# A Transformer Kernel's Last Down Projection in 1024-Column Superchunks, With a Third of Its k-Tile Pairs as Seven Block Products

## What is computed

```python
hn = _rms(x, norm_ffn[l])
x = x + ((jax.nn.silu(hn @ w_ffn_gate[l]) * (hn @ w_ffn_up[l])) @ w_ffn_down[l]).astype(x.dtype)
```

## Time and profile before

| | |
|---|---|
| median of 3 runs | 2681.32 us (2678.99 to 2684.05) |
| the profiled execution, first to last instruction | 2681.4 us |
| PE busy | 2611.9 us (97%), 12607 matmuls |
| DVE busy | 1574.9 us (59%) |
| ACT busy | 1212.8 us (45%) |
| DMA read | 562.39 MB, 211 GB/s over the span |
| chain that ended last | PE 88%, DVE 5%, DMA 5%, ACT 1% |

### The profile page before, as it was taken

How to read it: one execution, slowest core, us unless ns; L and a number is a source line. 1 busy time by engine, 2 the same in 40 slices (tenths; PEclk the granted TensorE clock), 3 DMA queues, 4 the chain that set the end, 5 groups by cost and what they waited for, 6 DMA issues and landing times.

```text
span 2681.4 us, 31852 instructions
## 1 busy us (share of the span) xinstructions
PE 2611.9 (97%) x12607; PEld 2149.9 (80%) x12607; DVE 1574.9 (59%) x1780; ACT 1212.8 (45%) x1634; POOL 10.8 (0%) x62
## 2 busy tenths in 40 slices
PE   5799999999999999999999999999999999999999
PEld 1478877888888888888888888888888888888887
DVE  0489768877545555555555775555555554455554
ACT  1245554544434444444445654544444444344443
POOL 0000000000000000000000000000000000000000
PEclk7799999999999999999999999999999999999999
DMA  9899639787555556555554674445556555565554
GB/s 390 334 345 330 202 141 366 268 284 273 187 190 188 188 188 204 188 188 189 183 178 151 205 245 141 126 164 182 185 181 199 181 195 189 196 193 190 188 188 141
DMA packets 264754, 566.14 MB, mean 211 GB/s; under 512 B 14271, under 2 KB 37564, under 8 KB 252092
## 3 DMA queue, kind: packets, MB, share of 16 engines
q1 hardware_dynamic: 262100, 562.88, 62.0%
q10 hardware_dynamic: 2538, 1.65, 0.2%
HBM read 562.39 MB, written 2.10 MB: 211 GB/s over the span
## 4 chain that ended last, share of the span: by engine, by line
PE 88%; DVE 5%; DMA 5%; ACT 1%; issue 1%; ACTq 0%; DVEq 0%
PE acc L492 66%; PE acc L3061 4%; PE acc L3064 2%; PE sc L3061 2%; DMA w_raw<-in_w_ada_dram 2%; PE tp L3061 2%; PE tp L531 2%; DVE w_lo L443 2%; DVE acc_ada L1663 2%; PE sc L3064 1%; PE tp L3064 1%; DMA w_raw<-in_w_in_dram 1%; PE acc L2729 1%; DMA w_raw<-in_w_out_dram 1%; PE sc L3233 1%
## 5 line engine op out<-in xcount | busy, mean ns | idle before, releaser
L443 DVE TENSOR_TENSOR w_lo<-w_raw,w_hi 128x1024 fp32r<-128x1024 f32 (+2 forms) x878 | 1053.3, 1217 | 581.4 <-ACT w_hi L438 573.8
L438 ACT ACTIVATE w_hi<-w_raw 128x1024 fp32r<-128x1024 f32 (+2 forms) x878 | 912.9, 1054 | 935.0 <-PE acc L492 657.4
L492 PE MATMUL acc<-w_hi,h_both 128*128 128x512 f32 (+2 forms) x3512 | 971.1, 392 | 13.0 <-DVE w_lo L443 8.5
L492 PEld LDWEIGHTS acc<-w_hi,h_both 128*128 128x128 f32 x3512 | 649.5, 188 | 146.5 <-DVE w_lo L443 9.5
L492 PE MATMUL acc<-w_lo,h_both 128*128 128x512 f32 (+2 forms) x1756 | 539.5, 388 | 0.0
L492 PEld LDWEIGHTS acc<-w_lo,h_both 128*128 128x128 f32 x1756 | 329.9, 188 | 68.1
L492 PE MATMUL acc<-w_hi,f_hi 128*128 128x512 f32 x864 | 268.5, 392 | 0.0
L492 PE MATMUL acc<-w_lo,f_hi 128*128 128x512 f32 x864 | 266.1, 389 | 0.0
L492 PE MATMUL acc<-w_hi,f_lo 128*128 128x512 f32 x864 | 266.0, 389 | 0.0
L492 PEld LDWEIGHTS acc<-w_hi,f_hi 128*128 128x128 f32 x864 | 161.6, 188 | 34.7 <-issue 1.2
L492 PEld LDWEIGHTS acc<-w_lo,f_hi 128*128 128x128 f32 x864 | 162.2, 188 | 33.9
(11 more groups left out here) (463 smaller groups left out, 2002.2 us busy)
## 6 DMA issues: line engine op xcount, KB each, us to landing
w_raw<-in_w_ff_dram SPq DMA_DIRECT2D x128, 1024.0 KB, 5.4
w_raw<-in_w_in_dram SPq DMA_DIRECT2D x108, 1024.0 KB, 5.1
w_raw<-in_w_ada_dram SPq DMA_DIRECT2D x96, 1024.0 KB, 7.4
w_raw<-in_w_ffn_gate_dram SPq DMA_DIRECT2D x44, 1024.0 KB, 5.1
w_raw<-in_w_ffn_up_dram SPq DMA_DIRECT2D x44, 1024.0 KB, 5.1
w_raw<-in_w_ffn_down_dram SPq DMA_DIRECT2D x44, 1024.0 KB, 5.0
w_raw<-in_w_out_dram SPq DMA_DIRECT2D x32, 1024.0 KB, 5.5
w_raw<-in_w_up_fox_dram SPq DMA_DIRECT2D x8, 1024.0 KB, 5.0
```

What stands on the lines that cost most here:

```text
L438: nc.scalar.activation(dst, src, ACT.Copy).then_inc(hi_done, 1)
L443: nc.vector.tensor_tensor(dst, src, hi.bitcast(F32), ALU.subtract).then_inc(lo_done, 1)
L492: last = nc.tensor.matmul(acc[b][:, t, 0:width], st[:, kt, t * P:(t + 1) * P], w[:, slot, kt - 2 * j, 0:width], start=(kt == 0 and n == 0) ...
```

## The change

The four column chunks of a group become two superchunks (`s`) of 1024 columns, each over all k-tile pairs of the group. A load is now two k-tiles x 1024 columns (still 1 MB). A superchunk's four outputs (2 token tiles x 2 column blocks) and four further products fill all eight banks.

Most pairs stay as they were, "eights": eight block products (2 token tiles x 2 k-tiles x 2 column blocks) of three matmuls, two halves of 12. They go to four banks, `sc[1]`, `acc[g][0]`, `acc[g][1]`, `sc[0]`, where g is the pair of the moment and u the other. Of the 12 (10) pairs of a group, 4 (3) are "sevens": seven products, of sums of activation blocks and sums of weight blocks (Winograd's form of Strassen's product), in four halves of 6, 6, 6 and 3 matmuls. They use the same four banks for three of them and `acc[u][0]`, `acc[u][1]`, `tp[0]`, `tp[1]` for the other four. The order of pairs is two eights and a seven in turn, then what is left, a seven last; in the last superchunk of all, the last two pairs are exchanged, so that an eight is last.

What comes with it:

- for each seven VectorE makes four 512-element sums of the weight blocks and seven block remainders in place of four; ScalarE makes seven block copies in place of four;
- for each chunk j that feeds a seven, ScalarE and VectorE make the activation sums during the gate and up products of chunk j + 1 (two 512-element copies, four 128-element sums, one 512-element remainder);
- at the end of a superchunk ScalarE copies all eight banks to `down_m` (3 copies behind the split of the next superchunk's or gate chunk's first half, 5 behind that of its second, `down_copies`), and VectorE adds them to `x` in seven instructions behind the splits of halves 2 to 6 (`down_adds`): two of 512 and five of 1024 elements;
- TensorE starts the first half of the next superchunk, or of the next group's first gate chunk, when both `acc[g]` banks are copied;
- the last superchunk is added by `down_last`, and the output leaves in three stores, the last two of 512 KB after the last matmul.

The diff, cut to its core (the tile placements, the sync engine's source patterns and renamed semaphores are left out):

```diff
+        def seven_pairs(size):
+            return list(range(1, 2 * (size - 2), 2))
+
+        def down_order(size, last):
+            seven = seven_pairs(size)
+            eight = [p for p in range(2 * size) if p not in seven]
+            order = []
+            for p in seven:
+                take = 2 if p != seven[-1] else len(eight)
+                order += [(q, False) for q in eight[:take]] + [(p, True)]
+                eight = eight[take:]
+            if last:
+                order[-2:] = order[:-3:-1]
...
-                weights(A["w_ffn_down_2"][0], 4, 4 * size, row0=f0 * CW, uniform=0)
+                for s in range(2):
+                    order, halves = down_order(size, f0 > 0 and s == 1)
...
+            def down_copies(idx, last, a, part):
...
+                if part == 0:
+                    act.wait_ge(S("down_added"), 7 * idx)
+                todo = (((0, 5, sc[1], copied), (1, 0, u_[:, 0, :], u_free), (1, 2, g_[:, 0, :], g_free)),
+                        ((2, 6, u_[:, 1, :], u_free), (2, 3, g_[:, 1, :], g_free), (3, 1, tp[0], copied),
+                         (3, 7, tp[1], copied), (4, 4, sc[0], copied)))[part]
+                for halves_gone, to, bank, free in todo:
+                    act.wait_ge(half_used, last + halves_gone)
+                    nc.scalar.activation(down_m[:, to, :], bank, ACT.Copy).then_inc(free, 1)
...
+                        if last and at == len(order) - 2:
+                            u = (n.acc + 1) % 2
+                            for nth, to in ((0, 0), (1, 6)):
+                                act.wait_ge(half_used, n.half + h0 + nth + 1)
+                                nc.scalar.activation(down_m[:, to, :], acc[u][:, nth, :], ACT.Copy).then_inc(acc_free[u], 1)
...
+            def down_adds(idx, s, a, k):
+                if k == 2:
...
+                    V.tensor_tensor(down_m[:, 1, :], down_m[:, 0, :], down_m[:, 1, :], ALU.add).then_inc(added, 1)
+                    dve.wait_ge(g_free, 2 * (a // 2) + 2)
+                    V.tensor_tensor(x_halves(0, s), x_halves(0, s), down_m[:, 2:4, :], ALU.add).then_inc(added, 1)
+                elif k == 3:
...
+                    V.tensor_tensor(down_m[:, 7, :], down_m[:, 1, :], down_m[:, 7, :], ALU.add).then_inc(added, 1)
+                    V.tensor_tensor(x_halves(1, s), x_halves(1, s), down_m[:, 4:6, :], ALU.add).then_inc(added, 1)
+                elif k == 4:
...
+                    V.tensor_tensor(x_halves(0, s), x_halves(0, s), down_m[:, 0:2, :], ALU.add).then_inc(added, 1)
...
+            def down_last(half, a, h_seven, h_eight):
...
+                dve.wait_ge(half_used, half + h_seven + 3)
+                dve.wait_ge(u_free, used + 1)
+                link(V.tensor_tensor(down_m[:, 1, :], down_m[:, 0, :], tp[0], ALU.add))
+                link(V.tensor_tensor(down_m[:, 7, :], down_m[:, 1, :], tp[1], ALU.add))
+                V.tensor_tensor(x_halves(0, 1), x_halves(0, 1), down_m[:, 0:2, :], ALU.add)
+                link(V.tensor_tensor(x_halves(1, 1), x_halves(1, 1), twice_wide(down_m[:, 7, :]), ALU.add))
+                dve.wait_ge(u_free, used + 2)
+                xr = x[:, :, 3 * CW:D]
+                link(V.tensor_tensor(xr, xr, twice_wide(down_m[:, 6, :]), ALU.add))
+                dve.wait_ge(half_used, half + h_eight + 2)
+                V.tensor_tensor(x_halves(0, 1), x_halves(0, 1), g_[:], ALU.add).then_inc(S("down_added"), 1)
+                V.tensor_tensor(x_halves(1, 1), x_halves(1, 1), sc_both[:], ALU.add).then_inc(S("down_added"), 1)
...
+                        V.tensor_tensor(sums_w[:, 1, :], block[:, 3, :], block[:, 1, :], ALU.subtract).then_inc(summed, 1)
+                        V.tensor_tensor(block[:, 1, :], block[:, 1, :], block[:, 0, :], ALU.subtract).then_inc(summed, 1)
+                        lo_half(0, block[:, 0:4:2, :])
+                        after(h0)
+                        dve.wait_ge(summed, 4 * sevens + 2)
+                        V.tensor_tensor(sums_w[:, 0, :], block[:, 3, :], block[:, 1, :], ALU.subtract).then_inc(summed, 1)
+                        lo_half(1, block[:, 1:4:2, :])
+                        after(h0 + 1)
+                        dve.wait_ge(summed, 4 * sevens + 3)
+                        V.tensor_tensor(block[:, 2, :], block[:, 2, :], sums_w[:, 0, :], ALU.subtract).then_inc(summed, 1)
+                        lo_half(2, sums_w[:])
+                        after(h0 + 2)
+                        lo_half(3, block[:, 2:3, :], 1)
+                        after(h0 + 3)
...
+                        if at == 0:
+                            pe.wait_ge(acc_free[n.acc % 2], 2 * (n.acc // 2))
...
+                        pe.wait_ge(lo_done, h.val(1))
+                        three(m1, both, 2 * pair, slice(0, P), h.slot(RING), 0, opens, ends)
+                        three(m2, both, 2 * pair + 1, slice(0, P), h.slot(RING), 1, False, closes).then_inc(half_used, 1)
+                        pe.wait_ge(lo_done, h.val(2))
+                        three(m5, form[0], nth, all_of, (h + 1).slot(RING), 0, opens, ends)
+                        three(m3, form[3], nth, all_of, (h + 1).slot(RING), 1, False, closes).then_inc(half_used, 1)
+                        pe.wait_ge(lo_done, h.val(3))
+                        if opens and s == 0:
+                            wait_hidden(use + 2 * (done + size))
+                        three(m6, form[1], nth, all_of, (h + 2).slot(RING), 0, opens, ends)
+                        three(m7, form[2], nth, all_of, (h + 2).slot(RING), 1, opens, ends).then_inc(half_used, 1)
+                        pe.wait_ge(lo_done, h.val(4))
+                        three(m4, both, 2 * pair + 1, slice(P, T), (h + 3).slot(RING), 0, False, closes).then_inc(half_used, 1)
```

More of the change, by code:

```diff
@@ L308, in build @@
         hid_banks = ((acc[1], sc_both), (acc[0], tp_both))
+        def seven_pairs(size):
[10 more added lines that the diff above has]
+                order[-2:] = order[:-3:-1]
+            out, half = [], 0
+            for p, is_seven in order:
+                out.append((p, is_seven, half))
+                half += 4 if is_seven else 2
+            return out, half
         row = {}
@@ L1563, in after_gate @@
                                 act_norm_first(jj)
+                            elif jj < 2:
+                                down_copies(1, n.half - 4, n.acc - 2, jj)
                         elif jj == 5:
-                            hidden_out(j + -1)
+                            hidden_out(j + -1, forms)
+                        elif jj == 7 and forms:
+                            act.wait_ge(S("forms_made"), j.times(4).val(4 * seven_before - 1))
+                            nc.scalar.activation(sf_hi[:, bass.ds((j + -1).val(), 1), :, :], f_sums[:].unsqueeze(1),
+                                                 ACT.Copy).then_inc(S("forms_copied"), 1)
                     def after_up(jj):
@@ L1594, in _, with after @@
                 n.acc += 2 * size
-                weights(4, 4 * size, lambda c: None, uniform=0,
-                        first=lambda j: hidden_out(At(size - 1)) if j == 5 else None)
+                for s in range(2):
+                    last = g == 1 and s == 1
+                    order, halves = down_order(size, last)
+                    def after(k):
+                        if s == 0:
+                            if k == 5:
+                                hidden_out(At(size - 1))
+                        elif k < 2:
+                            down_copies(2 * g, n.half - 4, n.acc - 2, k)
+                    for at, (pair, is_seven, h0) in enumerate(order):
+                        h, L = At(n.half + h0), At(n.load + at)
+                        block = raw[:, L.slot(RING)]
+                        if not is_seven:
+                            for j in range(2):
+                                split_hi(act, h + j, L, j, w_hi[:, (h + j).slot(RING)], block[:, 2 * j:2 * j + 2, :])
+                                after(h0 + j)
+                            continue
+                        split_hi(act, h, L, 0, w_hi[:, h.slot(RING)], block[:, 0:4:2, :])
+                        after(h0)
+                        act.wait_ge(S("w_summed"), 4 * sevens + 2)
+                        split_hi(act, h + 1, L, 1, w_hi[:, (h + 1).slot(RING)], block[:, 1:4:2, :])
+                        after(h0 + 1)
+                        act.wait_ge(S("w_summed"), 4 * sevens + 3)
+                        split_hi(act, h + 2, L, 1, w_hi[:, (h + 2).slot(RING)], sums_w[:])
+                        after(h0 + 2)
+                        act.wait_ge(S("w_summed"), 4 * sevens + 4)
+                        split_hi(act, h + 3, L, 1, w_hi[:, (h + 3).slot(RING), 0:1], block[:, 2:3, :])
+                        after(h0 + 3)
+                        sevens += 1
+                        if last and at == len(order) - 2:
[3 more added lines that the diff above has]
```

(8 more changed lines are left out.)

199 lines of the change are left out of this document (169 added, 30 removed).

## The result

| | before | after |
|---|---|---|
| median | 2681.43 us (2678.20 to 2684.82, 9 runs) | 2687.4 us (2684.95 to 2691.81, 9 runs) |
| profiled execution, span | 2681.4 us | 2683.0 us |
| last transposes of group 0 to the last add | 2225.30 us to its end: 452.92 us | 2220.43 us to its end: 459.39 us |
| TensorE in that stretch / last add behind the last matmul | 451.59 / 1.33 us | 456.72 / 2.67 us |

The ratio is 1.0021, interval [1.0011, 1.0030]: **slower by 6.0 us**. The forecast was slower by 14.0, to 2695.3; the time is in the range's lowest part.

What follows compares the result with a forecast made beforehand. The prediction took TensorE's unbroken matmuls, 0.2267 us each, to bound the kernel. It summed -9.5 + 6.6 + 11.4 + 2.2 + 1.3 + 2.0 = +14.0 us, to 2695.3 us on the median, range 2687 to 2702.

Steps and rivals of the forecast that it cites:

- the last eight: Last pair: TensorE waits 1.3 us because ScalarE copies two banks ahead of splitting it.
- the end: After the last matmul: VectorE's last adds end 3.1 to 3.2 us behind it instead of 1.26, costing 2.0 us.
- -9.5: Saving in the sevens: 42 matmuls fewer at 0.2267 us each, 9.5 us less.
- the two figures: Skill page's 512-column matmul times, 131 ns sustained and about 216 ns alone; by them the saving would be 5.5 or 9.1 us.
- The start of a superchunk: Second superchunks and group 1's first gate chunk: TensorE waits for ScalarE's bank copies, 3 x 2.2 us.
- The first seven of a second superchunk: Each group's second superchunk: delayed halves and the previous superchunk's adds make TensorE wait for VectorE, 2 x 5.7 us.
- first seven of a first superchunk: Each group's first superchunk: the seven's third half, made behind hidden_out, comes late, 2 x 1.1 us.
- The bounds: Whole change: +17.4 us with slower copies and 512-element work, +4.6 us if VectorE's SBUF work ran at one-operand pace.
- rival B: Half the cost is covered, by one-operand pace or free adds: 2684 to 2686 us, about no change; chance 9%.
- A: Ring covers nearly all, TensorE hardly waiting at sevens and starts: 2673.8 us, faster; chance 5%.
- C: Clock falls too, 1.6 us each at three starts and behind two slow sevens: 2700 to 2703 us; chance 6%.
- the 3.42 us at 100 us: Stretch without a matmul in the trace before, after which the clock is 0.50, 1.2 GHz; evidence for the falling clock.

Runs made afterwards that it cites:

- e6: Changed kernel plus one unread 1024-element VectorE addition behind half 5 of both second superchunks and the gate chunk between: 2696.84 us, one profile.
- e4: Changed kernel plus two unread 512-element ScalarE copies among the bank copies at each of the three starts: 2692.44 us, one profile.
- e5: Changed kernel with three additions moved behind the first seven, acc[g] copied first, and last copies, a weight sum and last additions reordered: 2680.97 us, ratio 0.9994.
- e8: e5 with all seven additions of the previous superchunk moved behind the first seven: 2676.54 us, ratio 0.9978 to the kernel before.
- e3: Changed kernel with all pairs as eights in 1024-column superchunks, using the same four banks each time: 2688.61 us, ratio 1.0019 to the kernel before.

## Why the prediction was wrong in size

**Right.** The direction, and the places where waits arise: three starts for ScalarE's bank copies, the first seven of every superchunk, the last eight and the end, with no other seven waiting; 12565 matmuls; 0.227 us a matmul in the sevens too, so -9.5; clock 1.00 throughout; no transfer in the way. On the pace of a matmul the trace was rightly preferred to the two figures that the prediction gives from the Trainium skill, page "TensorE: Matmul & The Clock Gate", section "Back-to-back issue gap".

**The steps that failed** are the sums at "The start of a superchunk" ("Sum 2 x 1.06 + 5 x 0.60 = 5.1"), at "The first seven of a second superchunk" ("VectorE then has 3 remainders (3.7), two adds of 0.69 and two of 1.22 (3.8) and two sums (1.4)", "= 3.1 against 1.36 of matmuls: 1.8 twice") and the like at the first seven of a first superchunk and the last eight. They add up what each instruction takes by itself, though on an engine that is never idle the next one starts before the last one's recorded end. From the end of a half to TensorE's release it was 4.4 us and not 5.1. For VectorE's work up to the seven's first half it was 8.2 (2277.63 to 2285.81) and not 8.9. For each of the next halves 2.87 and not 3.1. At the end the step failed only in part, since four of its seven additions wait for the one directly before: from TensorE's start of the last eight to the last add it was 8.4 and not 8.7, and TensorE took 5.8 and not 5.6.

**Why so small an error halved the result.** 7 to 13% on a row of work is much more on a wait, which is the difference of two rows: 1.14 + 0.60 + 1.14 - 1.36 is 1.5 where 1.8 stood, and the first half's wait of 1.0 vanished altogether. All places together, each such a difference, went from 23.5 to 15.6 us (14.2 of waits and 1.34 at the end), and the 9.5 saved were left against them. The bounds took other instructions' durations for the doubtful ones, up to +17.4 and down to +4.6; the measured +6.5 lies between them, but for another reason than the low end had, a faster form of instruction. That the time lies in the stated range at all is in part luck: its low end of 2687 was set with rival B in mind, not from any doubt about the sums.

**What would have told it.** The merged rows of before, "x2" and "x3" quoted above. In the same manner the prediction had told a matmul's duration, 0.39, from its pace, 0.227. The Trainium skill says it too: page "Perfetto Trace Analysis", section "Optimizing Scalar/DVE Operations", has the profiled duration hold a part, the write's acknowledgement, in which the next instruction is already under way. By its figures that part is about 60 ns for VectorE and 93 for ScalarE on SBUF. The traces here have 83 and 110 (copies of halves).

**The rivals.** A and B fall: the price of an addition on the critical row is its full distance of starts (e6), and every place paid. B's numbers (2684 to 2686) lie close to the result, but neither of its mechanisms is there: no place was free, and the durations are those of the two-operand rows. C is real, not in this kernel but one us of waiting away (e4 each time, e6 once of two), at the price it was given. That the price fits is in part luck. The prediction read a fall behind the 3.42 us at 100 us off, but in before the clock stands at 0.50 already from 83.3 us on, with TensorE busy 5.3 of 6.7 us there, and returns at 103.7: these rows show low speed and its end, not what began it.

## What to carry to other kernels

When work is stepped through on an engine that doesn't rest, count from start to start, which merged rows of the timeline give; durations are right for the last instruction before somebody else goes on, and for one that the very next instruction waits for. A wait is a difference of two long rows, so check its terms to a few per cent before adding several up. And work that nobody waits for (the additions here) belongs where its engine has room: moving three of them cost one line and was worth 6 us, the other four another 4 us (e5 to e8), while speeding up the earlier of two waits on one chain was given back at the second.

## What was not expected of the hardware

- Instructions that follow each other on VectorE start 0.08 us before the last one's recorded end, on ScalarE 0.10 to 0.17. A wait for a semaphore that an earlier instruction of the same engine raised costs nothing if another instruction stands between: the sums L2910 and L2914 and adds L2774 to L2786 have such waits and stand at the same distance as remainders without. Where an instruction waits for the one directly before it, the overlap is gone: it starts 0.03 us behind its end (0.72 and 1.25 apart, from L2793 to L2801 in after, from L2794 to L2808 in e8).
- Behind a wait of TensorE the second matmul starts 0.33 us after the first, 0.11 more than normal, and further ones 0.233 apart for a while, not 0.227.
- In this stretch the clock fell after idle times of 2.17 (three of three) and 2.35 us (one of two), and not after the 1.67 of e3: then some eight matmuls at 0.43 us, 1.6 us lost. One us more of waiting at such a place can cost 2.6. But the idle time alone doesn't decide. In the part ahead of the change, which does the same work in all ten profiles, the clock fell at the wait of 2.59 us (290 to 298 us) in three of them, at that of 2.41 (320 to 330) in five, at that of 2.26 (344 to 355) in all ten. It fell in all ten, too, between 473 and 483 us, around twelve transposes, where the longest wait is 1.77 in nine of them. What decides stays open.
